# All large SBUF buffers of a transformer-block kernel moved to multiples of 2048 bytes

## What is computed

```python
h = h + 0.5 * rmsnorm(swiglu(rmsnorm(h), w_gate, w_up, w_down))        # ffn1, inner width 2816
z = rmsnorm(h) @ w_in                                                  # then split in ten pieces
a  = mla_branch(c_q, c_kv, k_r, ...) @ w_branch_mla                    # 8 heads, softmax attention
bm = mlstm_branch(ml_q, ml_k, ml_v, ...) @ w_branch_ml                 # 4 heads, 2 directions, chunks of 128
h = h + rmsnorm((g_a * a + g_b * bm) @ w_out)
h = h + 0.5 * rmsnorm(swiglu(...))                                     # ffn2, same sizes as ffn1
h = h + rmsnorm(sigmoid(rmsnorm(h) @ ple_w_gate) * (p @ ple_w_proj))
```

## Time and profile before

| | |
|---|---|
| median of 3 runs | 1323.67 us (1323.06 to 1326.23) |
| the profiled execution, first to last instruction (span) | 1322.0 us |
| its own time | no separate record of it; its span lies 1.7 us under the median |
| PE busy | 1263.0 us (96%) |
| mean granted TensorE clock | 0.978 of 2.4 GHz |
| DVE, ACT, POOL busy | 678.4, 425.6, 118.5 us |
| moved by DMA | 107.75 MB |

### The profile page before, as it was taken

One profiled execution on the slowest core, in us unless ns is written; L12 is line 12 of the kernel. 1 busy time (PEld: TensorE's weight loads), 2 busy tenths in 40 slices (PEclk: granted clock), 3 DMA queues, 4 the chain that ended last, 5 costly groups with the idle time before them and its releaser, 6 DMA issues.

```text
span 1322.0 us, 15620 instructions
## 1 busy us (share of the span) xinstructions
PE 1263.0 (96%) x5909; PEld 1034.5 (78%) x5909; DVE 678.4 (51%) x1042; ACT 425.6 (32%) x612; POOL 118.5 (9%) x96
## 2 busy tenths in 40 slices
PE   5899999999997999999999999899999999999996
PEld 4688888888876877777788878778888888888785
DVE  5744444432247766744555566485444443222674
ACT  3432323321133433335321333243232332112452
POOL 3000000000024000000201200230000000000333
PEclk8899999999998999999999999999999999999897
DMA  6333333322231231110231123213332323223101
GB/s 187 85 106 95 95 96 95 103 95 90 94 74 29 68 112 48 49 32 17 80 96 33 49 80 96 80 48 114 93 105 86 111 81 109 96 95 105 39 32 64
DMA packets 95810, 107.75 MB, mean 82 GB/s; under 512 B 15030, under 2 KB 85398, under 8 KB 95766
## 3 DMA queue, kind: packets, MB, share of 16 engines
q1 hardware_dynamic: 95766, 107.15, 27.3%
HBM read 105.04 MB, written 2.10 MB: 81 GB/s over the span
## 4 chain that ended last, share of the span: by engine, by line
PE 87%; DVE 8%; ACT 2%; issue 2%; DMA 1%; SPq 0%; POOL 0%; DVEq 0%; ACTq 0%
PE bank L280 24%; PE bank L282 24%; PE bank L281 24%; PE bank L868 2%; PE bank L882 2%; DVE v_lo L453 1%; PE bank L408 1%; DVE tbuf L446 1%; PE bank L990 1%; PE bank L890 1%; PE bank L287 1%; PE bank L374 1%; DVE w_lo L310 1%; PE bank L289 1%; PE bank L288 1%
## 5 line engine op out<-in xcount | busy, mean ns | idle before, releaser
L310 DVE TENSOR_TENSOR w_lo<-w_raw,w_hi 128x1024 fp32r<-128x1024 f32 x195 | 241.9, 1246 | 395.0 <-ACT w_hi L303 386.9
L280 PE MATMUL bank<-v_hi,w_hi 128*128 128x512 f32 x968 | 381.0, 394 | 6.7 <-DVE w_lo L310 6.3
L282 PE MATMUL bank<-v_hi,w_lo 128*128 128x512 f32 x968 | 377.5, 390 | 0.0
L281 PE MATMUL bank<-v_lo,w_hi 128*128 128x512 f32 x968 | 377.1, 390 | 0.0
L303 ACT ACTIVATE w_hi<-w_raw 128x1024 fp32r<-128x1024 f32 x195 | 203.8, 1055 | 372.1 <-PE bank L282 368.5
L280 PEld LDWEIGHTS bank<-v_hi,w_hi 128*128 128x128 f32 x968 | 182.1, 188 | 44.7 <-DVE w_lo L310 6.6
L282 PEld LDWEIGHTS bank<-v_hi,w_lo 128*128 128x128 f32 x968 | 182.0, 188 | 38.4
L281 PEld LDWEIGHTS bank<-v_lo,w_hi 128*128 128x128 f32 x968 | 182.1, 188 | 37.5 <-issue 0.2
L282 PE MATMUL bank<-prod_hi,w_lo 128*128 (+1 forms) x352 | 139.0, 395 | 0.0
L280 PE MATMUL bank<-prod_hi,w_hi 128*128 (+1 forms) x352 | 139.0, 395 | 0.0
L281 PE MATMUL bank<-prod_lo,w_hi 128*128 (+1 forms) x352 | 139.0, 395 | 0.0
(11 more groups left out here) (268 smaller groups left out, 1419.7 us busy)
## 6 DMA issues: line engine op xcount, KB each, us to landing
w_raw<-in_ffn_w_gate SPq DMA_DIRECT2D x44, 512.0 KB, 3.8
w_raw<-in_ffn_w_up SPq DMA_DIRECT2D x44, 512.0 KB, 3.8
w_raw<-in_ffn_w_down SPq DMA_DIRECT2D x44, 512.0 KB, 3.4
w_raw<-in_w_in SPq DMA_DIRECT2D x32, 512.0 KB, 3.8
w_raw<-in_w_out SPq DMA_DIRECT2D x8, 512.0 KB, 3.4
w_raw<-in_ple_w_gate SPq DMA_DIRECT2D x8, 512.0 KB, 3.4
x_tm<-in_x SPq DMA_DIRECT2D x2, 1024.0 KB, 5.0
w_raw<-in_w_branch_mla SPq DMA_DIRECT2D x4, 512.0 KB, 3.4
```

What stands on the lines that cost most here:

```text
L280: nc.tensor.matmul(o, whi, a_hi, start=start, stop=False)
L281: nc.tensor.matmul(o, whi, a_lo, start=False, stop=False)
L282: return nc.tensor.matmul(o, wlo, a_hi, start=False, stop=stop)
L310: nc.vector.tensor_tensor(w_lo[:, s, :], w_raw[:, s, :], w_hi[:, s, :].bitcast(F32), ALU.subtract).then_inc(w_lo_done, 1)
```

## The change

The small tables come first, then the cursor is rounded up to a multiple of 2048, then the large buffers follow; `ident` goes behind the shared area. `ones` shrinks from 128 columns to 2, and L946 reads its first column broadcast over 128; `small` shrinks from 320 to 288 columns. Nothing else is edited: no instruction, wait or transfer is added, removed or reordered.

```diff
+    cols = sb("cols", [P, NVEC])
+    small = sb("small", [P, 288])
+    ones = sb("ones", [P, 2])
+    cursor[0] = (cursor[0] + 2047) // 2048 * 2048
     h = sb("h", [P, KD, S])
     v_hi = sb("v_hi", [P, KD, S], F32R)
     v_lo = sb("v_lo", [P, KD, S], F32R)
     w_raw = sb("w_raw", [P, RING, CH])
     w_hi = sb("w_hi", [P, RING, CH], F32R)
     w_lo = sb("w_lo", [P, RING, CH], F32R)
-    ident = sb("ident", [P, P])
-    ones = sb("ones", [P, P])
-    cols = sb("cols", [P, NVEC])
     r_b = sb("r_b", [P, S])
     sqacc = sb("sqacc", [P, S])
     scratch = sb("scratch", [P, 4, S])
-    small = sb("small", [P, 320])
     A0 = cursor[0]
     KB = 1024
-    assert A0 + 97 * KB <= nc.sbuf_usable_end, (A0, nc.sbuf_usable_end)
+    assert A0 % 2048 == 0
+    ident = at("ident", [P, P], F32, A0 + 97 * KB)
+    assert A0 + 97 * KB + 512 <= nc.sbuf_usable_end, (A0, nc.sbuf_usable_end)
...
-            last = nc.tensor.matmul(B[3][:, 32 * d:32 * d + 32], ones[0:8, :], D8[d][0:8, :], start=True, stop=True)
+            last = nc.tensor.matmul(B[3][:, 32 * d:32 * d + 32], ones[0:8, 0:1].broadcast_to([8, P]), D8[d][0:8, :], start=True, stop=True)
```

More of the change, by code:

```diff
@@ L209, in scol @@
         used[0] += n
-        assert used[0] <= 320
+        assert used[0] <= 288
         return small[:, a:a + n]
```

## The result

The changed kernel takes 1318.11 us in the median of 5 runs (1314.45 to 1319.53), the kernel before, in the same comparison, 1323.67 (1322.09 to 1326.29). The ratio of the two is 0.9937 with a 95% interval of 0.9922 to 0.9952. By the ratio that is 8.3 us less (1323.67 x 0.0063), between 6.4 and 10.3. The two medians alone lie 5.6 us apart, outside that interval: five runs spread over 4 to 5 us. The experiments bear the ratio out and not the 5.6. With their comparisons there are 43 runs of the kernel before, 1325.4 us in the mean; the five of the changed kernel have a mean of 1317.4, so 8.0 us less. The profiled execution has a span of 1312.5 us, 9.5 under that of before.

The account below looks back on a forecast made before the run. PE's own pace in the weight products was taken as the bound; 7.0 us (`prod`) + 1.5 (`cq`, `oT`, `bT`, `pT`) = 8.5 off the 1322.0 span gives 1313.5, plus 1.7 makes 1315.2 us; forecast's own range 1312 to 1319, overall 1309 to 1325.

Parts of the forecast that it names:

- That PE's pace decides in the weight products: Weight products: ACT waited 368.5 us for PE, so shorter transfers, rounding or subtraction gain nothing there.
- That the distance of the two operands sets the pace: All matmuls: pairs a multiple of 512 bytes apart take 226.7 ns, pairs 128 over that 233.3.
- `prod`, 7.0 us: Down stages: 1056 matmuls go from 233.3 to 226.7 ns, all of it shortening the path, 7.0 us.
- `cq`, `oT`, `bT`, `pT`, 1.5 of 2.0 us: Matmuls with these tiles also reach the fast pace; 1.5 of 2.0 us counted, as vector work and handshakes lie between.
- Fast pairs: 3288 matmuls already at 226.7 ns keep their distance: 0 taken, between 21.7 us of loss and 44.0 of gain.
- ACT, DVE, transfers, `ones`, 0: Other engines, weight transfers and the smaller `ones` table: placement and shorter fill taken to gain 0.
- Rival 1: Slow pace belongs to the upper buffer space from 129792 on, so nothing moves: 1323.7 us, chance 0.15.
- Rival 2: Pair (0, 0) is itself bad: the 3288 fast matmuls go to 233.3 ns, time 1345 us, chance 0.06.
- rival 3: Rows crossing a multiple of 2048 cost time; without crossings all go towards 213.3 ns, about 1252 us, chance 0.07.
- Rival 4: Only multiples of 2048 count, so .5 KB tiles at 512 stay slow: 7.0 us remain, 1316.7, inside the forecast.
- The step itself: Distance between moving and stationary operands: the fast pace was put at multiples of 512 bytes.
- two read streams that meet in SBUF: PE's reads of moving operand and next stationary block meet, losing 13.3 or 20 ns per matmul at 2.4 GHz.

Follow-up runs that it names:

- experiment 1: Kernel before with only `small` cut from 320 to 288 columns, moving the shared area down 128 bytes: ratio 0.9945 to the kernel before, 1317.64 us beside 1325.35.
- experiment 2: Changed kernel with the shared area alone shifted by 128 bytes: ratio 1.0001 to the kernel before.
- (7): Changed kernel with 384 bytes skipped ahead of `w_raw`, moving weights and shared area against `v`: ratio 1.0047 to the kernel before.
- Experiment 3: Kernel of fp32r matmuls alone, distance between weights and moving rows varied from 0 to 496 bytes: 226.7 ns per matmul at 0, 233.4 at 64.
- experiment 6: Matmul-only fp32r kernel with narrower weight blocks and shorter rows: at distance 0, 226.7 ns with 128 columns, 231.7 with 32; 119.8 with 256-column rows.
- Experiment 8: Matmul-only kernel comparing types over distances: fp32r 226.7 to 233.4 ns with block and row fixed, bf16 215 to 216, float32 429.2 per pass.

## Why the prediction was right

The time came out 8.3 us (0.63%) lower by the ratio, forecast 8.5 (0.64%). The median itself is 1318.11, 2.9 us over the forecast 1315.2 and inside the 1312 to 1319 that the forecast gave itself. Its steps:

- **That PE's pace decides in the weight products:** right. PE's busy time fell by 9.4 us and the span by 9.5, and ACT still waits 361.0 us for PE, where it had waited 368.5.
- **That the distance of the two operands sets the pace:** right, and shown in both directions: by moving the area alone (experiment 1), by undoing that alone (2), and by moving the weights (7). Experiment 3 shows it with matmuls alone, so no other engine's work is needed for it.
- **`prod`, 7.0 us:** measured 3.5 + 3.5 = 7.0.
- **`cq`, `oT`, `bT`, `pT`, 1.5 of 2.0 us:** the stretch between the down stages, with `cq`, `oT` and `bT`, lost 1.4 us. The end lost 1.3, but nearly all of that is the clock: it was granted at 1.2 GHz for 3.4 us there in place of 6.8. `pT` takes 13.31 us from first to last start after the change and 14.23 before it, and 13.45 in experiment 2, which has the slow distance and 3.4 us at the low clock. So the distance is worth some 0.1 us in `pT`, and 7.0 + 1.4 + 0.1 = 8.5 in the whole profile. Since experiment 2 has the shorter stretch with the slow layout, it is not the layout that sets it, as far as these runs show. So 9.5 of one profile and 8.3 of the runs don't contradict each other.
- **Fast pairs, 0 between a loss of 21.7 and a gain of 44.0:** right; `v` stands at 226.7 in both.
- **ACT, DVE, transfers, `ones`, 0:** right.
- **Rival 1 (0.15)** fell in experiments 1 and 2. So did, for fp32r, what the prediction drew from the Trainium skill (SBUF — State Buffer, "Who interferes with whom"), where PE has two independent read ports and never waits on anyone: that no placement can change the pace. 226.7 and 233.3 differ by an address alone. Whether it is those two ports that meet is not shown. For bf16 placement made no difference here (215 to 216 ns at every distance). **Rival 2** (the pair 0, 0 is a bad one) and **rival 3** (crossing a 2048 boundary costs) both fell with the changed kernel's own profile and with experiment 3.
- **Rival 4** (only multiples of 2048 count) fell too: `cq` and `bT`, now at 512, take 226.7 and 226.9. **The step itself was put too wide.** The period isn't 512, but 256 in all but one of the pairs tried. The trace of before couldn't tell 256 from 512, since all its pairs were either 0 or 128 over a multiple of 512.

What failed is the picture behind the step in the form in which experiment 6 tested it, though no number hung on it: two read streams that meet in SBUF, with a loss in proportion to the block. At distance 0 a narrower block lost more and not less (231.7 ns with 32 columns against 226.7), and with rows of 256 columns distance 128 cost nothing over distance 0 (118.8 against 119.8). What the loss is, and what in it repeats every 256 bytes, stays open.

## What to carry to other kernels

In a kernel bound by fp32r matmuls, put the moving rows and the weight blocks a multiple of 256 bytes apart; here this is worth 6.6 ns of 233.3, or 2.8% of each such matmul at 2.4 GHz, and costs a line in the layout. Not every other distance is slow, but none was faster. Read the pace of matmuls from start to start, tile by tile: two tiles that go through the same helper at different paces can point to their addresses. For bf16 and float32 nothing was to be won this way at the distances tried.

## What the runs showed of the hardware

- No group of fp32r at the 2.4 GHz level has a pace of 213.3 ns for 512 columns: 226.7 at the best distance tried, 234.3 at the worst. bf16 is at 215.8. The Trainium skill (TensorE: Matmul & The Clock Gate, "Wait — 56ns, not 53.3ns?") gives 215.7 ns for back-to-back matmuls of 512 columns. Experiment 8 agrees for bf16; the fp32r groups do not.
- At the 1.2 GHz level the same fp32r matmul takes 426.7 ns at the bad distance, which is 512 columns and nothing more. The changed kernel's `pT`, now at a good distance, takes 1.28 / 3 = 426.7 there as well, so at that level the distance made no difference:

```profile
1227.42 0.63 PE L282 MATMUL bank<-pT_hi,w_hi 128*128 128x512 f32 x1
...
1228.70 0.63 PE L282 MATMUL bank<-pT_hi,w_hi 128*128 128x512 f32 x1
```

- The slow paces are repeating patterns. With `prod` before the change, starts are 229 and 238 ns apart in turn; with `oT` seven different steps repeat. At a good distance it can take some ten matmuls from a break until the steps are even (experiment 6). Only the mean of several starts may be compared.
- A narrower weight block at the good distance is slower, not faster: 231.7 ns with 32 columns against 226.7 with 128.
